# Attention slots of a second block: value tiles beside softmax rows, one output projection behind all slots

## The chip, the cores and the metric

The kernel runs on one core of one Trainium2 chip. The metric is the device time of one execution in microseconds (us). The program issues work to TensorE (PE, matmuls and its weight loads PEld), VectorE (DVE), ScalarE (ACT), GpSimd (POOL) and SyncE (SP, DMA issues). Each engine runs its own queue in program order, and they meet at semaphores.

## The reference, cut to what matters

Two model blocks stand one behind the other, for 512 tokens of width 1024 in fp32. The first (two layers of gated feed-forward and a mixer) is not touched by the change. The second takes its output, normalises it, projects it, and runs a state-space branch and an attention branch side by side:

```python
h = rmsnorm_2(x, norm_mix); proj = h @ w_in
z, xBC, dt_raw, qkv, gate_logits = split(proj)
y_ssm = mamba2_branch(z, xBC, dt_raw, ...) @ w_ssm_out     # dt = softplus(dt_raw + dt_bias), causal conv of xBC, 4 groups
q, k = rope(qkv[0]), rope(qkv[1]); v = qkv[2]               # 12 heads of 128: 3 groups of 4
# per group: window 128, 512 (dilation 4), 2048 (dilation 16), softmax over its window;
# the three groups of a head are merged by a softmax over their log-sum-exp
y_att = dilated_attention_branch(q, k, v) @ w_att_out       # 4 merged heads, 512 -> 1024
mixed = sigmoid(gates[0]) * y_ssm + sigmoid(gates[1]) * y_att
x = x + mixed @ w_mix_out; then a gated feed-forward and a last rmsnorm
```

## The kernel before, in words

**Weights.** All weights lie in one list of blocks of 128 x 1024 fp32 (512 KB), in the order in which they are used (`second_blocks`, L2510, and `slot_blocks`, L2485, put the second block's together). SP loads them into four `raw` buffers (L425). GpSimd splits each block into a rounded high part `w_hi` (L445) and a remainder `w_lo` (L448), in two buffers; a split begins when PE starts on the next block (semaphore `w_begun`). `product` (L495) multiplies one 128x128 tile of a block with 512 columns in three matmuls: high by high (L499), high by low (L503), low by high (L504). `project` is one block: eight products, 24 matmuls, into one PSUM bank of 128x512.

**Entry of the second block** (`second_mixer` of each engine). PE projects the dt tile into bank 5, adds up squares with a ones matmul (L518), projects three value tiles, with a second sum of squares between them. DVE forms two reciprocal roots (`first_rms`, `rstd`), the raw dt rows (L2263, L2265), scales the turn tables (L2268), scales and copies the value tiles to `att_vt` in residue order (L2037), then runs the softplus of dt (the "dt chain", L2273 to L2282, with ACT's exponential and logarithm), and clears `att_sum` (L2284).

**Slots.** A slot is one merged head: four of them, slots 0 to 2 in a loop, slot 3 behind it. Its steps:

- six tiles (three query, three key) into a ring of seven banks (5, 6, 7, 0, 1, 2, 3) with `tile_free` for each. DVE rotates each one: two products with the turn tables and a third (L2053 to L2055), then an add into `att_qk` (L2057);
- 12 transposes of the value tiles (L944), copied by ACT (L1452, behind a table load);
- four softmax rows r. Scores (L955, L958, banks r mod 2 and 2 + r mod 2), DVE's `shift` (scale and mask L2063 and L2065, maximum L2067, negation L2068), ACT's exponential (L1456), DVE's `over_sum` (L2073, L2074), PE's six transposes into banks 5 and 6 (L969), ACT's copies (L1463, L1465), and the mix of values in bank 7 (L979). Scores of r + 1 are issued ahead of the transposes of r; a value tile of the next slot (bank 4) stands between transposes and mix of r = 0, 1, 2. The softmax buffers are two deep;
- DVE normalises two of the eight tiles of x (`normalise`, L2046), ACT rounds the mixed output (L1471), DVE takes the remainder `att_lo` (L2089);
- PE waits for it and multiplies by this head's rows of `w_att_out` (`accumulate`, one block, eight bank results); DVE adds each to `att_sum` (L2027).

**Tail.** Behind slot 3 PE transposes the dt rows (L1134), ACT copies them and loads `sel`, and PE projects six state-space tiles into banks 5, 6, 7 in turn (`fill_bank`, `proj_free`). DVE scales each into `xbc_pad` (L2099) and runs a convolution of four taps (L2113 and three of L2116). Then come four state-space groups (`ssm_group`). Order is fixed by hand in every queue; no planner sets it.

Of the kernel before, what the change touches and what calls it, by code (L numbers as in the profile page):

```python
# [18 lines left out]
F32 = mybir.dt.float32  # L19
# [63 lines left out]
SLOT_STEPS = {  # L83
    "pe": {"w_split": 10, "tile_free": 9, "vt_ready": 3, "v_timed": 3, "soft_ready": 4, "soft_copied": 4,
           "soft_tail": 4, "soft_shifted": 4, "att_split": 1, "acc_free": 8, "qk_ready": 6},
    "act": {"v_turned": 3, "soft_shifted": 4, "soft_turned": 8, "att_mixed": 1},
    "dve": {"acc_free": 8, "tile_free": 9, "dve_step": 18, "tile_ready": 9, "soft_in": 4,
           "soft_shifted": 4, "soft_exp": 4, "soft_ready": 4, "att_rounded": 1, "att_split": 1,
           "acc_ready": 8, "qk_ready": 6},
}  # L90
# [76 lines left out]
def build(nc, io):  # L167
    ctx = ExitStack()
    with ctx:
# [11 lines left out]
        VALUE_BANKS = (3, SUM_BANK, 5)  # L181
# [93 lines left out]
        att_sum = sb("att_sum", [P, DC, T], F32, two_mem)  # L275
        ssm_sum = sb("ssm_sum", [P, DC, T], F32, two_mem)
# [17 lines left out]
        att_hi = sb("att_hi", [P, T], F32R, att_mem)  # L294
        att_lo = sb("att_lo", [P, T], F32R, att_mem)
# [71 lines left out]
        acc_ready, acc_free = sem("acc_ready"), sem("acc_free")  # L367
# [114 lines left out]
        def _(pe):  # L482
# [13 lines left out]
            def product(out, s, t, hi, lo, start, stop):  # L496

                hi_w, lo_w = w_hi[:, s, t * P:(t + 1) * P], w_lo[:, s, t * P:(t + 1) * P]
                first = nc.tensor.matmul(out, hi_w, hi, start=start, stop=False)  # L499
                if fresh[0]:  # L500
                    first.then_inc(w_begun, 1)
                    fresh[0] = False
                nc.tensor.matmul(out, hi_w, lo, start=False, stop=False)  # L503
                return nc.tensor.matmul(out, lo_w, hi, start=False, stop=stop)  # L504

# [400 lines left out]
            def accumulate(hi, lo, tiles):  # L906

                per = BLOCK // tiles
                for m in range(DC):
                    if m % per == 0:  # L910
                        s = take()
                    pe.wait_ge(acc_free, c.next(acc_free))
                    for k in range(tiles):
                        last = product(bank[m % 4][:], s, (m % per) * tiles + k, hi[k], lo[k],
                                       k == 0, k == tiles - 1)
                    last.then_inc(acc_ready, 1)

            def ring_tiles(n_tiles):
                for n in range(n_tiles):
                    if n == 3:  # L920

                        pe.wait_ge(acc_free, c.at(acc_free) + 4)
                    pe.wait_ge(tile_free, c.next(tile_free))
                    project(bank[RING[n % len(RING)]][:]).then_inc(tile_ready, 1)

            def value_tile(b):

                pe.wait_ge(tile_free, c.next(tile_free))

                pe.wait_ge(tile_free, c.at(tile_free) + len(RING) - 1)  # L930
                project(bank[b][:]).then_inc(tile_ready, 1)

            def attention_slot(more):

                pe.wait_ge(tile_free, c.at(tile_free) + len(RING))
                ring_tiles(2 * GROUPS)

                pe.wait_ge(vt_ready, c.next(vt_ready, GROUPS))
                for g in range(GROUPS):
                    if VALUE_BANKS[g] == RING[0]:  # L940

                        pe.wait_ge(tile_free, c.at(tile_free) + len(RING) + 1 - 2 * GROUPS)
# [3 lines left out]
                    last.then_inc(v_turned, 1)  # L946
                pe.wait_ge(v_timed, c.next(v_timed, GROUPS))

# [13 lines left out]
                scores(0)  # L962
                for r in range(RES):
                    if r + 1 < RES:
                        scores(r + 1)
# [6 lines left out]
                    if more and r < GROUPS:  # L972

                        value_tile(SUM_BANK)
# [8 lines left out]
                pe.wait_ge(att_split, c.next(att_split))  # L983
                accumulate([att_hi[:]], [att_lo[:]], 1)
# [14 lines left out]
            def out_block(waits=0):  # L999
# [4 lines left out]
                for m in range(2):  # L1004
                    to = fill_bank()
                    for k in range(4):
                        last = product(to[:], s, 4 * m + k, ssm_hi[:, k, :], ssm_lo[:, k, :], k == 0, k == 3)
# [108 lines left out]
            def second_mixer():  # L1116
                pe.wait_ge(tile_free, c.next(tile_free))

                project(bank[RING[0]][:], arriving=1).then_inc(tile_ready, 1)
                sum_squares()  # L1120
                for b in RING[1:1 + GROUPS]:
                    pe.wait_ge(tile_free, c.next(tile_free))
                    project(bank[b][:]).then_inc(tile_ready, 1)
                    if b == RING[1]:
                        sum_squares(1)
                with c.loop(3, SLOT_STEPS["pe"]):
                    attention_slot(True)
                attention_slot(False)
                pe.wait_ge(acc_free, c.at(acc_free) + 4)
# [9 lines left out]
                for n in range(SSM_TILES):  # L1139
# [1485 lines left out]
```

## Time and profile before

| what | value |
|---|---|
| runs, median | 3560.83 us (three: 3555.93 to 3565.5) |
| profiled execution | 3557.09 us, its span 3555.3 us |
| PE busy | 3309.0 us (93%) |
| DVE busy | 1814.8 us (51%) |
| POOL busy | 1827.6 us (51%) |
| ACT busy | 757.1 us (21%) |
| granted PE clock, mean | 0.969 of full |

The span is the time from the first to the last recorded instruction; the execution's own time has 1.8 us more. Busy PE time overstates PE's work, since matmuls overlap in their pipeline; a row's idle time and what ended it say more. "[2.44 <-DVE square_sum L1592]" behind a row reads: the engine sat idle for 2.44 us before it, and DVE's instruction at L1592 released it. "x12" is the number of instructions that a row stands for.

### The profile page before, as it was taken

What the parts mean: (1) busy time and instruction counts of PE and PEld (TensorE: products, weight loads), DVE (VectorE), ACT (ScalarE), POOL (GpSimd) and SP (SyncE); (2) the same over time, 40 slices, a digit from 0 to 9 for tenths busy, and PEclk for the clock granted to TensorE, in tenths of its full rate; (3) what the DMA queues carried; (4) which work ended last, traced back from release to release, by engine and by line L of the source; (5) the groups of instructions that cost most, each with busy time, mean ns of one, the idle gap of its engine ahead of it and who ended that gap; (6) DMA issues with size and microseconds to landing.
All of it is one profiled execution on the core that took longest, in us unless ns stands there. A gap on an engine that the chain in (4) does not pass through costs nothing.

```text
span 3555.3 us, 44605 instructions
## 1 busy us (share of the span) xinstructions
PE 3309.0 (93%) x14288; PEld 2589.9 (73%) x14288; DVE 1814.8 (51%) x2100; ACT 757.1 (21%) x1269; POOL 1827.6 (51%) x1026
## 2 busy tenths in 40 slices
PE   7999997899999999997889999888898899999997
PEld 5788774478887788874457888666776677778886
DVE  6541267663313733157654331755668866853313
ACT  2110124422201110013432210211113222222201
POOL 4556650056666646661036666433354445666664
PEclk9999998999999999998899999999999999999998
DMA  4223320023333223331013333321222222233332
GB/s 139 77 78 97 109 81 15 5 74 100 94 95 117 85 71 95 95 107 31 12 42 91 98 95 95 103 60 59 59 75 66 60 66 72 88 94 95 95 95 76
DMA packets 77138, 280.90 MB, mean 79 GB/s; under 512 B 9351, under 2 KB 9735, under 8 KB 76361
## 3 DMA queue, kind: packets, MB, share of 16 engines
q1 hardware_dynamic: 74016, 268.84, 25.1%
q10 hardware_dynamic: 2984, 10.27, 0.9%
q8 instruction: 82, 1.34, 0.2%
q14 instruction: 56, 0.45, 0.0%
HBM read 276.97 MB, written 2.10 MB: 78 GB/s over the span
## 4 chain that ended last, share of the span: by engine, by line
PE 78%; DVE 14%; issue 5%; ACT 2%; DVEq 0%; ACTq 0%; DMA 0%; SPq 0%
PE bank L499 23%; PE bank L504 23%; PE bank L503 23%; DVE xbc L2116 1%; PE bank L763 1%; PE bank L706 1%; PE bank L624 1%; DVE x_lo L1582 1%; PE bank L781 1%; DVE ssm_lo L1736 1%; DVE square_sum L1592 1%; DVE scaled L1947 1%; PE bank L979 1%; DVE y L1824 1%; DVE reach L2198 1%
## 5 line engine op out<-in xcount | busy, mean ns | idle before, releaser
L445 POOL TENSOR_SCALAR w_hi<-raw 128x1024 fp32r<-128x1024 f32 x504 | 551.2, 1094 | 1648.3 <-PE bank L499 1641.2
L448 POOL TENSOR_TENSOR w_lo<-raw,w_hi 128x1024 fp32r<-128x1024 f32 x504 | 1264.0, 2508 | 42.0
L499 PE MATMUL bank<-x_hi,w_hi 128*128 128x512 f32 x2896 | 1158.8, 400 | 83.2 <-DVE x_lo L1582 30.2
L504 PE MATMUL bank<-x_hi,w_lo 128*128 128x512 f32 x2896 | 1141.2, 394 | 0.0
L503 PE MATMUL bank<-x_lo,w_hi 128*128 128x512 f32 x2896 | 1140.9, 394 | 0.0
L499 PEld LDWEIGHTS bank<-x_hi,w_hi 128*128 128x128 f32 x2896 | 552.5, 191 | 224.3 <-issue 95.4
L503 PEld LDWEIGHTS bank<-x_lo,w_hi 128*128 128x128 f32 x2896 | 553.0, 191 | 118.9 <-issue 5.1
L504 PEld LDWEIGHTS bank<-x_hi,w_lo 128*128 128x128 f32 x2896 | 551.7, 190 | 118.2
L504 PE MATMUL bank<-hidden_hi,w_lo 128*128 (+1 forms) x880 | 347.6, 395 | 0.0
L499 PE MATMUL bank<-hidden_hi,w_hi 128*128 (+1 forms) x880 | 347.6, 395 | 0.0
L503 PE MATMUL bank<-hidden_lo,w_hi 128*128 (+1 forms) x880 | 347.6, 395 | 0.0
L1602 DVE SCALAR_TENSOR_TENSOR x<-bank,x 128x512 f32<-128x512 f32 x64 | 43.4, 686 | 561.8 <-PE bank L504 561.2
L1617 DVE TENSOR_TENSOR up<-bank,rstd 128x512 f32<-128x512 f32 x110 | 76.1, 692 | 396.5 <-PE bank L504 390.3
L1621 DVE TENSOR_TENSOR hidden_lo<-hidden,hidden_hi 128x512 f32 (+1 forms) x110 | 163.9, 1490 | 113.3 <-ACT hidden_hi L1185 113.3
L503 PEld LDWEIGHTS bank<-hidden_lo,w_hi 128*128 128x128 f32 x880 | 165.2, 188 | 40.2
L504 PEld LDWEIGHTS bank<-hidden_hi,w_lo 128*128 128x128 f32 x880 | 165.2, 188 | 40.1
L499 PEld LDWEIGHTS bank<-hidden_hi,w_hi 128*128 128x128 f32 x880 | 165.2, 188 | 40.1
L1169 ACT ACTIVATE x_hi<-x,gains 128x512 fp32r<-128x512 f32 x72 | 51.7, 718 | 644.2 <-DVE x L1602 643.3
L1185 ACT ACTIVATE hidden_hi<-hidden 128x512 f32 (+1 forms) x110 | 69.5, 632 | 477.5 <-DVE hidden L1619 477.5
L1183 ACT ACT_TABLE_LOAD x68 | 87.2, 1283 | 243.8 <-DVE gate L1615 243.8
L1619 DVE TENSOR_TENSOR hidden<-gate_silu,up 128x512 f32<-128x512 f32 x110 | 119.1, 1083 | 36.1 <-DVE up L1617 26.3
L1615 DVE TENSOR_TENSOR gate<-bank,rstd 128x512 f32<-128x512 f32 x110 | 76.1, 691 | 96.6 <-PE bank L504 86.3
(368 smaller groups left out, 3258.3 us busy)
## 6 DMA issues: line engine op xcount, KB each, us to landing
raw<-in_w SPq DMA_DIRECT2D x504, 512.0 KB, 3.6
dft<-in_dft ACTq DMA_DIRECT2D x2, 1536.0 KB, 6.8
x<-in_x SPq DMA_DIRECT2D x2, 1024.0 KB, 6.7
out<-x SPq DMA_DIRECT2D x4, 512.0 KB, 2.6
mask<-in_mask ACTq DMA_DIRECT2D x1, 1536.0 KB, 7.2
filt_cos<-in_dft_filter ACTq DMA_DIRECT2D x2, 512.0 KB, 6.5
filt_sin<-in_dft_filter ACTq DMA_DIRECT2D x2, 512.0 KB, 7.7
sel<-in_sel ACTq DMA_DIRECT2D x1, 768.0 KB, 4.4
```

The source lines that it names most:

```text
L445: nc.gpsimd.tensor_scalar(w_hi[:, s % 2, :], raw[:, s, :], 1.0, 0.0, ALU.mult, ALU.add).then_inc(w_rounded, 1)
L448: nc.gpsimd.tensor_tensor(w_lo[:, s % 2, :], raw[:, s, :], w_hi[:, s % 2, :].bitcast(F32), ALU.subtract).then_inc(w_split, 1)
L499: first = nc.tensor.matmul(out, hi_w, hi, start=start, stop=False)
L503: nc.tensor.matmul(out, hi_w, lo, start=False, stop=False)
L504: return nc.tensor.matmul(out, lo_w, hi, start=False, stop=stop)
L1169: nc.scalar.activation(x_hi[:, m, :], x[:, m, :], ACT.Copy, scale=g).then_inc(x_rounded, 1)
L1183: nc.scalar.activation(gate_silu[:], gate[:], ACT.Silu).then_inc(gate_activated, 1)
L1185: nc.scalar.activation(to, hidden[:], ACT.Copy).then_inc(hidden_rounded, 1)
L1615: link(nc.vector.tensor_tensor(gate[:], bank[2 * b][:], rstd[:], ALU.mult), gate_scaled)
L1617: link(nc.vector.tensor_tensor(up[:], bank[2 * b + 1][:], rstd[:], ALU.mult), pair_free)
L1619: link(nc.vector.tensor_tensor(hidden[:], gate_silu[:], up[:], ALU.mult), hidden_ready)
L1621: link(nc.vector.tensor_tensor(to_lo, hidden[:], to_hi.bitcast(F32), ALU.subtract), hidden_split)
```

## The change

- Entry: the first value tile is projected ahead of the first sum of squares, the third is split in two parts around the second. The sums go to banks 3 and 2. PE waits for no ring. DVE leaves the reciprocal of `first_rms` to slot 0 and scales the turn tables behind the value tiles. The dt chain, the logarithm of ACT and the clearing of `att_sum` leave this place.
- Slots: written out four times, no loops. Query and key tiles go to banks 0 to 5 without `tile_free`. Value transposes go to banks 6, 7, 3. The next slot's value tiles all use bank 4: tile 0 behind the value transposes, tile 1 behind the scores of rows 0 and 1, tile 2 between transposes and mix of row 2. In slot 3 the first state-space tile stands behind the scores of rows 0 and 1. Scores of r + 2 are issued behind the transposes of r.
- `att_hi` and `att_lo` have room for four heads, which share memory with tensors that are first written later. The output product of a slot is gone; behind slot 3 come one state-space tile and then four blocks of `w_att_out` that sum over all four heads in PSUM (`out_block`). DVE copies eight results to `att_sum` in place of 32 adds.
- The dt chain stands behind slot 3, with two convolutions and the first copies of the output between its steps. Four state-space tiles follow the dt transposes, not six.

```diff
             def attention_slot(j):
+                more = j < 3
+                for n in range(2 * GROUPS):
+                    if n == VALUE_TILE_BANK:
+                        pe.wait_ge(vt_ready, c.next(vt_ready, GROUPS))
+                    project(bank[n][:]).then_inc(tile_ready, 1)
+                pe.wait_ge(att_split, c.next(att_split))
+                pe.wait_ge(qk_ready, c.at(qk_ready) + VALUE_BANKS[2] + 1)
                 for g in range(GROUPS):
...
+                def beside(n):
+                    if more:
+                        if n:
+                            pe.wait_ge(vt_ready, c.at(vt_ready) + n)
+                        project(bank[VALUE_TILE_BANK][:]).then_inc(tile_ready, 1)
+                pe.wait_ge(qk_ready, c.at(qk_ready) + VALUE_TILE_BANK + 1)
+                beside(0)
                 pe.wait_ge(v_timed, c.next(v_timed, GROUPS))
                 pe.wait_ge(qk_ready, c.next(qk_ready, 2 * GROUPS))
...
                 scores(0)
+                scores(1)
+                if more:
+                    beside(1)
+                else:
+                    project(bank[VALUE_TILE_BANK][:]).then_inc(tile_ready, 1)
                 for r in range(RES):
-                    if r + 1 < RES:
-                        scores(r + 1)
                     pe.wait_ge(soft_ready, c.next(soft_ready))
...
-                    if more and r < GROUPS:
-                        value_tile(SUM_BANK)
+                    if r + 2 < RES:
+                        scores(r + 2)
+                    if r == 2:
+                        beside(2)
                     pe.wait_ge(soft_copied, c.next(soft_copied))
...
-                pe.wait_ge(att_split, c.next(att_split))
-                accumulate([att_hi[:]], [att_lo[:]], 1)
             def second_mixer():                                  # PE
+                project(bank[5][:], arriving=1).then_inc(tile_ready, 1)
+                project(bank[6][:]).then_inc(tile_ready, 1)
+                sum_squares(FIRST_SUM_BANKS[0])
+                project(bank[7][:]).then_inc(tile_ready, 1)
+                s = take()
+                project_part(bank[VALUE_TILE_BANK][:], s, 0, 2)
+                sum_squares(FIRST_SUM_BANKS[1])
+                project_part(bank[VALUE_TILE_BANK][:], s, 2, DC).then_inc(tile_ready, 1)
+                pe.wait_ge(both_means, 1)
+                pe.wait_ge(rms_ready, 3 * LAYERS + 1)
+                for j in range(4):
+                    attention_slot(j)
+                proj_tile()
+                pe.wait_ge(att_split, c.next(att_split))
+                for m in range(0, DC, 2):
+                    out_block(hi=att_hi, lo=att_lo)
                 pe.wait_ge(dt_done, c.next(dt_done, 2))
...
-                for n in range(SSM_TILES):
+                for n in range(2, SSM_TILES):
                     proj_tile()
             def attention_slot(j):                               # DVE, behind the six tiles
+                if more:
+                    value_tile(0, VALUE_TILE_BANK)
                 shift(0)
+                shift(1)
                 over_sum(0)
+                over_sum(1)
+                if more:
+                    value_tile(1, VALUE_TILE_BANK)
+                shift(2)
+                over_sum(2)
+                shift(3)
+                over_sum(3)
+                if more:
+                    value_tile(2, VALUE_TILE_BANK)
+                if j == 0:
+                    link(nc.vector.reciprocal(first_rms[:], first_rms[:]))
                 normalise(2 * j)
                 normalise(2 * j + 1)
...
-                add_outputs(att_sum)
+            def att_output(m):
+                b = bank[FILL[projected[0] % len(FILL)]]
+                projected[0] += 1
+                dve.wait_ge(proj_ready, c.next(proj_ready))
+                nc.vector.tensor_copy(att_sum[:, m, :], b[:]).then_inc(proj_free, c.add(proj_free))
             def second_mixer():                                  # DVE, behind the slots
+                link(nc.vector.tensor_scalar(u, e, 1.0, None, ALU.add), dt_log)
+                link(nc.vector.memset(xbc_pad[:, :, 0:SSM_TAPS - 1], 0.0))
+                dve.wait_ge(tile_ready, c.next(tile_ready))
+                link(nc.vector.tensor_tensor(xbc_pad[:, 0, SSM_TAPS - 1:], bank[VALUE_TILE_BANK][:], rstd[:],
+                                             ALU.mult))
+                conv_taps(0, 0)
+                conv_tile(1)
+                conv_taps(0, 1)
+                att_output(0)
                 dve.wait_ge(dt_magnitude, c.next(dt_magnitude))
                 link(nc.vector.tensor_scalar(spare, u, 1.0, None, ALU.subtract))
                 link(nc.vector.tensor_tensor(e, e, spare, ALU.subtract))
+                att_output(1)
                 link(nc.vector.reciprocal(u, u))
+                att_output(2)
                 link(nc.vector.tensor_tensor(e, e, u, ALU.mult))
                 link(nc.vector.tensor_tensor(log, log, e, ALU.add))
+                att_output(3)
...
+                for m in range(4, DC):
+                    att_output(m)
 def second_blocks(i):
...
+    first = group_tiles(w_x, w_b, w_c, 0)
+    out += first[0:2] + group_out(i["w_att_out_2"][0], 0) + first[2:]
```

## Rows read from the trace of the kernel before

**Rows 1.** Page, part 4: shares of the chain that ended last.
```profile
PE 78%; DVE 14%; issue 5%; ACT 2%; DVEq 0%; ACTq 0%; DMA 0%; SPq 0%
```

**Rows 2.** Windows: length; PE, PEld, DVE, ACT, POOL busy; PEclk, DMA share, GB/s.
```profile
2242.04:2271.87 29.83, 20.06 (x77) 14.86 (x77) 24.74 (x22) 12.02 (x17) 10.66 (x6) 0.92 0.35 131
2271.87:2361.70 89.83, 77.85 (x348) 63.15 (x349) 59.90 (x68) 11.64 (x22) 34.76 (x20) 0.89 0.20 59
2361.70:2444.44 82.74, 72.99 (x349) 59.57 (x348) 49.33 (x62) 11.06 (x21) 34.45 (x20) 0.96 0.21 59
2444.44:2526.16 81.72, 73.47 (x348) 59.84 (x349) 49.14 (x62) 11.06 (x21) 34.47 (x20) 0.96 0.21 63
2526.16:2595.28 69.12, 57.48 (x277) 46.16 (x275) 47.78 (x62) 11.05 (x21) 24.16 (x14) 0.95 0.18 54
2595.28:2632.21 36.93, 35.07 (x153) 28.84 (x153) 27.62 (x27) 6.10 (x9) 22.30 (x12) 0.95 0.34 104
```

**Rows 3.** PE's waits, 2240 to 2633 us: in total, times, longest.
```profile
PE bank L969 <- DVE soft L2074: 14.1, 5, 3.9
PE bank L955 <- DVE att_qk L2057: 10.5, 3, 5.5
PE bank L499 <- DVE att_lo L2089: 8.3, 4, 2.4
PE bank L979 <- ACT soft_t L1465: 6.2, 7, 0.9
```

**Rows 4.** Timeline of PE, entry and slot 3: start, length, idle before.
```profile
2244.47 1.12 PE L518 MATMUL bank<-square_sum,ones 128*128 128x512 f32 x2 [2.44 <-DVE square_sum L1592]
...
2254.11 2.08 PE L518 MATMUL bank<-square_sum,ones 128*128 128x512 f32 x2 [3.03 <-DVE square_sum L1592]
...
2271.87 0.76 PE L499 MATMUL bank<-x_hi,w_hi 128*128 128x512 f32 x1 [4.31 <-DVE att_vt L2037]
...
2562.47 1.13 PE L955 MATMUL bank<-att_qk 128*128 128x512 f32 x2 [2.15 <-ACT att_v L1452]
...
2570.86 2.90 PE L979 MATMUL bank<-soft_t,att_v 128*128 128x128 f32 x12 [0.71 <-ACT soft_t L1465]
```

**Rows 5.** Timeline of PE in mid-stream, slots 0 and 1.
```profile
2338.68 1.50 PE L979 MATMUL bank<-soft_t,att_v 128*128 128x128 f32 x12
...
2347.47 1.50 PE L979 MATMUL bank<-soft_t,att_v 128*128 128x128 f32 x12
...
2394.37 1.47 PE L944 MATMUL bank<-ident,att_vt 128*128 128x128 f32 x12
```

**Rows 6.** Timeline of POOL in slot 1.
```profile
2367.75 1.06 POOL L445 TENSOR_SCALAR w_hi<-raw 128x1024 fp32r<-128x1024 f32 x1 [1.94 <-PE bank L499]
2368.89 2.39 POOL L448 TENSOR_TENSOR w_lo<-raw,w_hi 128x1024 fp32r<-128x1024 f32 x1
2373.19 1.06 POOL L445 TENSOR_SCALAR w_hi<-raw 128x1024 fp32r<-128x1024 f32 x1 [1.91 <-PE bank L499]
```

**Rows 7.** Timeline of DVE on entry.
```profile
2247.76 6.30 DVE L1592 TENSOR_TENSOR square_sum<-square_sum,square 128x512 f32<-128x512 f32 x6
...
2274.46 3.34 DVE L2277 RECIPROCAL dt_rows<-dt_rows 32x512 f32<-32x512 f32 x1
```

**Rows 8.** Timeline of DVE, slots 1 and 3.
```profile
2369.71 2.53 DVE L2057 TENSOR_TENSOR att_qk<-rot 128x512 f32<-128x512 f32 x1
...
2575.57 0.69 DVE L2063 SCALAR_TENSOR_TENSOR soft<-bank,mask 128x512 f32<-128x512 f32 x1 [2.59 <-PE bank L958]
...
2580.03 0.69 DVE L2063 SCALAR_TENSOR_TENSOR soft<-bank,mask 128x512 f32<-128x512 f32 x1
```

**Rows 9.** Two lines' instructions: shortest, median, longest in ns.
```profile
L2057 DVE TENSOR_TENSOR att_qk<-rot x24: 1035/2526/3119, 2287.4 to 2561.2; 128x512 f32<-128x512 f32 x24
L2074 DVE TENSOR_SCALAR soft<-soft,soft_max x16: 619/620/1631, 2321.6 to 2583.8; 128x768 f32<-128x768 f32 x16
```

**Rows 10.** Groups of DVE, 2595 to 2632 us: busy, mean ns, idle before.
```profile
L2116 DVE SCALAR_TENSOR_TENSOR xbc<-xbc_pad,cols,xbc 128x512 f32<-128x512 f32 x13 | 17.3, 1332 | 0.5
```

More of the change, by code:

```diff
@@ L504, in product, with project_part @@
                 return nc.tensor.matmul(out, lo_w, hi, start=False, stop=stop)
+            def project_part(out, s, first, end):
+                for k in range(first, end):
+                    last = product(out, s, k, x_hi[:, k, :], x_lo[:, k, :], k == 0, k == DC - 1)
+                return last
             def project(out, arriving=0):
@@ L904, in _, with attention_slot @@
                 ffn()
[L906 to L938, printed above, removed]
+            def attention_slot(j):
+                more = j < 3
[5 more added lines that the diff above has]
+                pe.wait_ge(qk_ready, c.at(qk_ready) + VALUE_BANKS[2] + 1)
                 for g in range(GROUPS):
-                    if VALUE_BANKS[g] == RING[0]:
-                        pe.wait_ge(tile_free, c.at(tile_free) + len(RING) + 1 - 2 * GROUPS)
                     for t in range(RES):
@@ L1432, in second_mixer @@
                 act.wait_ge(sum_ready, c.next(sum_ready))
-                nc.scalar.activation(first_rms[:], bank[SUM_BANK][:], ACT.Sqrt, bias=eps[:], scale=1.0 / D
+                nc.scalar.activation(first_rms[:], bank[FIRST_SUM_BANKS[0]][:], ACT.Sqrt, bias=eps[:], scale=1.0 / D
                                      ).then_inc(rms_ready, 1)
@@ L1445, in second_mixer @@
                                      ).then_inc(dt_magnitude, 1)
-                act.wait_ge(dt_log, c.next(dt_log))
-                nc.scalar.activation(dt_rows[:, 3, :], dt_rows[:, 2, :], ACT.Ln).then_inc(dt_magnitude, 1)
-                with c.loop(4, SLOT_STEPS["act"]):
+                for j in range(4):
                     for g in range(GROUPS):
@@ L2019, in mixer @@
                 absorb(stage + 1, 1.0)
-            def add_outputs(total, first=False):
-                for m in range(DC):
-                    dve.wait_ge(acc_ready, c.next(acc_ready))
-                    if first:
-                        link(nc.vector.tensor_copy(total[:, m, :], bank[m % 4][:]), acc_free)
-                    else:
-                        link(nc.vector.tensor_tensor(total[:, m, :], total[:, m, :], bank[m % 4][:], ALU.add), acc_free)
             def by_residue(v):
@@ L2077, in attention_slot @@
                 shift(0)
+                shift(1)
                 over_sum(0)
-                for r in range(RES):
-                    if r + 1 < RES:
-                        shift(r + 1)
-                    if r + 1 < RES:
-                        over_sum(r + 1)
-                    if more and r < GROUPS:
-                        value_tile(r, SUM_BANK)
+                over_sum(1)
[9 more added lines that the diff above has]
+                    link(nc.vector.reciprocal(first_rms[:], first_rms[:]))
                 normalise(2 * j)
@@ L2283, in second_mixer @@
                      dt_done)
-                link(nc.vector.memset(att_sum[:], 0.0))
-                with c.loop(3, SLOT_STEPS["dve"]) as j:
-                    attention_slot(j, True)
-                attention_slot(3, False)
+                for m in range(4, DC):
+                    att_output(m)
                 dve.wait_ge(dt_timed, c.next(dt_timed))
                 link(nc.vector.memset(a_rows[:].bitcast(F32), 0.0))
-                link(nc.vector.memset(xbc_pad[:, :, 0:SSM_TAPS - 1], 0.0))
-                for k in range(SSM_TILES):
+                for k in range(2, SSM_TILES):
                     conv_tile(k)
```

96 lines of the change are left out of this document (38 added, 58 removed).

## The prediction

> **What bounds the kernel now.** I read the chain of waits first: TensorE (PE) holds 78% of it [rows 1], so time is won only where PE waits or runs below full clock. Then I cut the stretch that the change touches, from the first block's last product (2242.04 us) to the first state-space group (2632.21), into stages: entry, attention slots 0 to 3 (each with its output product), tail. They take 390.2 us, at a granted clock of 0.89 to 0.96 [rows 2]: part of it ran at 1.2 instead of 2.4 GHz. The list of PE's waits names what ends them: normalised softmax rows (14.1 us), rotated queries and keys (10.5), the rounding remainder att_lo of a slot's output (8.3), copies of turned probabilities (6.2 in 7) [rows 3]. PE's own timeline adds the entry (2.44, 3.03, 4.31) and shows what follows a wait: the mix at 2570.86, in slot 3 with its many waits, takes 2.90 us [rows 4], where one in mid-stream takes 1.50 [rows 5]. That is the lower clock.
>
> **What the stretch costs without waits.** In mid-stream GpSimd starts a new weight split each 5.44 us (2367.75, 2373.19), one a block [rows 6], so a projection tile, which is one block, is 5.44. From one mix to the next is 8.79 with a value tile inside [rows 5]: one softmax row (scores, transposes, mix) costs PE 8.79 − 5.44 = 3.35. The 12 value transposes show 1.47, of which 0.16 overlaps: 1.3 [rows 5]. The change keeps every block: 3 value tiles on entry, 24 query and key tiles, 9 value tiles, 4 blocks of output weights, 6 state-space tiles, 46 × 5.44 = 250.2; 16 rows 53.6; 4 × 1.3 = 5.2; two sums 1.8; dt transposes 0.7. Together 311.5, so 78.7 of the 390.2 us are waits and lower clock: the most that can be won.
>
> **Entry.** Now one tile stands ahead of the first sum, one and a quarter behind it, and no ring wait before slot 0. PE: 2242.0 + 5.4 + 0.9 + 5.4 + 1.4 = 2255.2. VectorE's (DVE) last six adds of squares end at 2254.1 [rows 7], and its chain begins 2.8 us later because the first sum does: 2256.9; up to 2259.5 if one more split falls on them. I take 2257.5: PE waits 2.4 (1.7 to 4.3), then 0.9 for the sum and 4.1 for three quarters of a tile: slot 0 begins at 2263 against 2271.87. The reciprocal of first_rms, the dt chain with its own (3.34 [rows 7]) and the memset of att_sum leave DVE's path to the first rotated tile. DVE still has the reciprocal of rstd (3.4), the dt rows, three value tiles and the turn tables, and comes to that tile some 3 us late. That lag ends at no wait of PE, since nothing in the six tiles waits for DVE.
>
> **A slot with a successor (0 to 2).** Value tile 0 covers the last rotation and ScalarE's (ACT) table load and value copies, for which PE waited 2.15 in slot 3 and more in the others [rows 3, 4]. Score sets 0 and 1 stand ahead of value tile 1. From a row's shift to the next is 4.46 in slot 3 [rows 8], the exponential's wait of 1.3 inside, and a normalisation is 0.62 [rows 9] with 0.2 for its reciprocal, which leaves a shift 2.3. From the end of scores 0 DVE needs two shifts and a normalisation: 5.5. PE has 1.35 + 5.44 = 6.8 of work: covered. And row 2 is ready 4.5 after scores 2, and PE has mix 0, transposes 1, scores 3, mix 1 = 4.65 meanwhile: covered by a hair. Row 3 lies under value tile 2. What stays is the last row's wait for its copies, 0.9 (6.2 / 7 [rows 3]). The wait of 2.2 to 2.4 us for att_lo goes: it is made under the next slot's first tile, and what is late next is nothing before the value transposes. Slot: 9 × 5.44 + 1.3 + 13.4 + 0.9 = 64.6; I take 65.1, three times 195.3. DVE is busy 49 us of 82 in slots 1 and 2 [rows 2], and eight adds of the output leave it: under 50 of 65.
>
> **Slot 3.** It has no value tiles; one state-space tile is put behind scores 1. The 2.2 after the value transposes stays [rows 4]; rows 0 and 1 are covered; row 2 waits 0.9 for copies; row 3 waits 1.6 (4.5 less transposes 0.66, copies 0.9, mix 1.34) and 0.9. 7 × 5.44 + 1.3 + 13.4 + 2.2 + 3.4 = 58.4.
>
> **Tail.** The output projection has the same 96 matmuls. DVE's 32 adds become 8 copies of 0.69, the time of a 128x512 read of a bank [rows 8]. Ahead of and between them DVE has two convolutions and the dt chain. A convolution is the bank's read and four steps of at most 1.33 on average [rows 10], 6.0 in all. PE fills three banks in turn with halves of 2.72. Counted from slot 3's last mix: att_lo and small steps 2.1, two convolutions 12.0, copy 0.7: bank free at 14.8, wanted at 13.6: wait 1.2. Then dt steps 1.8, copy 0.7, reciprocal 3.3, copy 0.7: free at 21.3, wanted at 20.2: wait 1.1. One tile 5.4, four blocks 21.8, these 2.3, transposes 0.7, dt_time 0.9, four tiles 21.8: 52.9. ACT's logarithm brings a table load more, which no PE work waits for; the load of sel comes behind dt_turned as before, beside four tiles. SP's weight queue and GpSimd's splits have the same number of blocks in another order: 0.
>
> **Unrolling.** PE, DVE and ACT now run the slots without a loop. Nearest rows: slots 0 to 2 (looped) and slot 3 (written out); the latter's chains are no longer [rows 4]. Gain inside covered chains: 0; code loading from 0 to 1 us a slot: I take 0.
>
> **Sum.** 21.0 + 195.3 + 58.4 + 52.9 = 327.6, plus 3 for lower clock. (Before, one minus the granted share times each stage's length is some 24 us, much of it while idle [rows 2]; waits over 2 us remain only on entry and in slot 3; bounds 0 and 8.) 330.6 against 390.2: −59.6. The profiled execution took 3557.1 us, span 3555.3 and 1.8 around it; it becomes 3497.5. The runs' median is 3.7 above it, so I say 3500. Its own range: 3489 to 3512.
>
> **The shared port, against this change.** The rotating add that starts at 2369.71 beside the split of 2368.89 + 2.39 takes 2.53 us and ends 0.96 behind the split's end [rows 6, 8]; at its shortest it takes 1.04, and a row's normalisation 0.62 or up to 1.63 [rows 9]. The Trainium skill, "SBUF — State Buffer", in its rule on the port pair that DVE shares with GpSimd, calls this an exclusive lock: the later one blocks for the whole instruction. The trace agrees: 0.96 is about the add's whole time alone. By that rule denser splits would lengthen DVE's covered chains by up to a split's 2.4 us each, which is rival A's mechanism; without any such meeting the sum stays as it is.
>
> **Rivals.** (A) Partly given back. A normalisation that meets a split is 1.0 longer [rows 9] and all behind it is later; 2 us twice in each slot (16), 8 more in the tail where convolutions and dt steps meet splits: +24, 3524. For it: row 2's cover has 0.1 us to spare. Against: these steps stand mostly where PE begins no block. 16%. (B) Waits only move, and all 78.7 come back: 3557. Against: each of the seven added covers holds 5.44 us of independent work. 3%. (C) Slower: DVE bounds the rotated tiles. It has them done in 4.9 of 5.44 us when the add meets a split (three steps of 0.7 and 2.5 [rows 8, 9]). If every add missed a split and waited for the next, a tile would cost DVE 10.9, and the six would lag 33 us per slot. It decides from 15 us of lag a slot (4 × 15 = the gain); at 17, 3497.5 + 68 = 3565. Against: once PE waits no split starts and the add takes 1.04, so the lag heals. By the port rule the same. 3%. (D) Weights come late: 0.5 MB in 5.44 us is 96 GB/s; the tail moved 104 [rows 2]. 3540, 1%. (E) No residual waits, full clock: 3487, 5%. My forecast: 72%.
>
> **How the numbers follow.** 8 in 10: 3486 to 3522, which leaves out most of A's far half, B, C, D and a little of E. No change means within 0.3%, about 10.7 us, the least a measurement of this kernel can tell. Faster: forecast, A, D and E, 94%; same, B, 3%; slower, C, 3%.
>
> **What would show it.** PE's waits in the stretch for DVE's soft rows fall from 14.1 to 2 to 4 us, for att_qk from 10.5 to under 1, for att_lo to 0; slots 65 us apart; granted clock near 1 in slots 0 to 2; two new waits near 1 us of an output half-block for a DVE copy. Wrong if a slot takes over 70 us, if tiles wait for weights, or if the tail takes over 58.

## The result, and the profile after

| | before | after |
|---|---|---|
| median | 3559.39 us (four runs, 3555.93 to 3565.5) | 3498.27 us (four runs, 3496.48 to 3501.54) |
| profiled execution, its span | 3557.09, 3555.3 | 3500.01, 3497.9 |
| PE, DVE busy | 3309.0, 1814.8 | 3284.9, 1804.6 |
| granted PE clock, mean | 0.969 | 0.977 |

Ratio of the medians 0.9831, 95% interval 0.9816 to 0.9845: 61 us faster. The forecast was 3500 (8 in 10: 3486 to 3522).

The windows of the changed kernel by stage, in the columns of [rows 2]: entry, slots 0 to 3, tail with the output projection.

```profile
2234.90:2259.18 24.28, 19.87 (x77) 15.04 (x76) 19.34 (x14) 7.95 (x11) 11.45 (x6) 0.93 0.43 160
2259.18:2325.86 66.68, 64.14 (x326) 53.05 (x324) 51.92 (x59) 11.81 (x23) 31.92 (x18) 1.00 0.23 72
2325.86:2392.63 66.77, 64.21 (x328) 53.12 (x326) 47.46 (x57) 9.66 (x20) 32.09 (x18) 1.00 0.22 71
2392.63:2459.39 66.76, 64.21 (x327) 53.12 (x326) 45.47 (x54) 9.67 (x20) 31.63 (x18) 1.00 0.23 71
2459.39:2519.02 59.63, 53.96 (x279) 44.21 (x278) 41.14 (x51) 9.66 (x20) 24.14 (x14) 1.00 0.20 62
2519.02:2572.34 53.32, 51.33 (x227) 40.91 (x226) 41.80 (x43) 8.49 (x12) 32.60 (x18) 1.00 0.30 94
```

The stretch takes 337.4 us where it took 390.2 [rows 2]: −52.7. The clock stands at 1.00 in all four slots. PE's waits in it (in total, times, longest), against [rows 3]:

```profile
PE bank L956 <- DVE soft L2054: 7.0, 5, 1.7
PE bank L518 <- DVE square_sum L1581: 4.4, 1, 4.4
PE bank L967 <- ACT soft_t L1452: 4.2, 5, 0.8
PE bank L938 <- DVE att_qk L2035: 2.1, 1, 2.1
PE bank L494 <- DVE att_sum L2116: 1.1, 2, 0.9
PE bank L494 <- ACT dt_time L1465: 0.9, 1, 0.9
```

Soft rows 14.1 to 7.0, rotated tiles 10.5 to 2.1 (slot 3 alone), att_lo 8.3 to none; the two sums' 5.5 became one wait of 4.4. All waits of over 0.15 us together fell from 53.2 to 19.7, by 33.5. The other 19.2 us of the 52.7 go with the clock (its mean in the stretch was 0.94 and is 0.99) and with what a wait costs beyond its listed time.

The spans differ by 57.4. The other 4.7 us lie outside the stretch: the changed kernel came to it 7.1 us ahead and lost 2.5 behind it. The code ahead of the stretch is the same in both. One place shows a part of it, the same PE work in the first block, before and then after, 20.40 us at a granted clock of 0.83 and 17.39 at 1.00:

```profile
1711.68:1732.08 20.40, 17.35 (x61) 9.45 (x59) 16.56 (x29) 9.75 (x20) 3.45 (x2) 0.83 0.18 53
```
```profile
1707.81:1725.20 17.39, 14.34 (x61) 8.75 (x59) 15.59 (x27) 8.78 (x18) 3.44 (x2) 1.00 0.21 62
```

### The profile page after: what moved, and what is told of

Read it like the earlier page. It is cut to its first block, busy times and chain, and to the rows that moved or that the text cites. A ratio compares the mean times of both kernels' runs of the same rounds, so it can differ in the third digit from the quotient of the medians.

```text
span 3497.9 us, 43803 instructions
## 1 busy us (share of the span) xinstructions
PE 3284.9 (94%) x14288; PEld 2575.5 (74%) x14288; DVE 1804.6 (52%) x2075; ACT 751.7 (21%) x1265; POOL 1832.2 (52%) x1026
## 4 chain that ended last, share of the span: by engine, by line
PE 80%; DVE 13%; issue 4%; ACT 2%; DVEq 0%; ACTq 0%; DMA 0%; SPq 0%
PE bank L494 24%; PE bank L499 24%; PE bank L498 24%; DVE xbc L2101 1%; PE bank L706 1%; PE bank L763 1%; DVE x_lo L1571 1%; PE bank L624 1%; DVE reach L2189 1%; PE bank L781 1%; DVE scaled L1936 1%; DVE square_sum L1581 1%; DVE y L1813 1%; DVE ssm_lo L1725 0%; PE bank L601 0%
## 5 line engine op out<-in xcount | busy, mean ns | idle before, releaser
L1591 DVE SCALAR_TENSOR_TENSOR x<-bank,x 128x512 f32<-128x512 f32 x64 | 43.5, 687 | 561.6 <-PE bank L499 561.0
```

## The experiments

Spans of different executions differ by such clock drops, so each kernel is judged twice: by its median against the kernel before, timed beside it, and by the **stretch**, the time from the start of GpSimd's weight split number 312 to that of number 368 (2207.78 to 2663.16 us before: 455.4). It is wider than the 390.2 us of [rows 2], and each kernel has the same blocks there. A repeat of the changed kernel gave the stretch to 0.01 us, the medians of its two sets differ by 4.

| kernel | median of its runs | ratio to before, 95% | stretch against before |
|---|---|---|---|
| changed | 3498.27 | 0.9831 (0.9816 to 0.9845) | −52.7 |
| e11, changed again | 3502.19 | 0.9848 (0.9826 to 0.9869) | −52.7 |
| e1, before without loops | 3542.7 | 0.9959 (0.9941 to 0.9976) | −10.7 |
| e2, output in the slots | 3517.81 | 0.9882 (0.9865 to 0.9898) | −37.8 |
| e2b, the same, dt later | 3516.76 | 0.9885 (0.9863 to 0.9907) | −37.5 |
| e3, row order undone | 3526.04 | 0.9908 (0.9891 to 0.9924) | −29.9 |
| e10, scores one row ahead | 3502.9 | 0.9842 (0.982 to 0.9864) | −49.6 |
| e4, entry undone | 3515.11 | 0.9872 (0.9855 to 0.9888) | −43.5 |
| e5, exponential 1 early | 3498.28 | 0.9826 (0.9803 to 0.985) | −59.6 |
| e6, e5 and tile 2 parted | 3490.15 | 0.9809 (0.9787 to 0.9831) | −63.2 |
| e7, second sum later | 3504.51 | 0.9849 (0.9829 to 0.9869) | −53.9 |
| e8, e6 and e7 | 3484.48 | 0.9798 (0.9776 to 0.9821) | −67.1 |
| e9, no remainder splits | 3492.51 | 0.9819 (0.9798 to 0.984) | −58.6 |

**e1.** The slot loops of the kernel before (slots 0 to 2 on PE and DVE, all four on ACT), written out.

```diff
-                with c.loop(3, SLOT_STEPS["pe"]):
+                for j in range(3):
```

> The kernel before, with its three inner slots written out instead of looped; nothing else changes. My theory of the forecast: the short pauses of 0.14 to 0.33 us that VectorE had between its steps in the looped slots come from the loop, and they go: per slot three exposed waits fall by 0.34, 0.63 and 0.66 us, 1.6 us in all, times 3 slots, so about 5 us less than before, 3554 us. Rival 1 (the loop itself was what the old slots lost): 15 us or more less, 3545 us or below. Rival 2 (longer code has its own price): no gain or slower than before.

Measured: 15 us by the medians, 10.7 by the stretch. The steps of a softmax row on DVE, in slot 0, looped and then written out:

```profile
2317.28 0.69 DVE L2063 SCALAR_TENSOR_TENSOR soft<-bank,mask 128x512 f32<-128x512 f32 x1 [3.20 <-PE bank L958]
2318.12 0.42 DVE L2065 SCALAR_TENSOR_TENSOR soft<-bank,mask 128x256 f32<-128x256 f32 x1
2318.69 0.95 DVE L2067 TENSOR_REDUCE soft_max<-soft 128x1 f32<-128x768 f32 x1
```
```profile
2315.15 0.69 DVE L2063 SCALAR_TENSOR_TENSOR soft<-bank,mask 128x512 f32<-128x512 f32 x1 [3.15 <-PE bank L958]
2315.88 0.42 DVE L2065 SCALAR_TENSOR_TENSOR soft<-bank,mask 128x256 f32<-128x256 f32 x1
2316.34 0.95 DVE L2067 TENSOR_REDUCE soft_max<-soft 128x1 f32<-128x768 f32 x1
```

A step begins 0.15 us behind the end of the one before it in the loop, 0.04 behind it now. PE's wait for att_lo in slots 1 and 2 went from 2.36 and 2.23 to 1.48. A slot from last mix to last mix went from 83.97 and 82.13 to 77.80 and 79.19; slot 0 gained 0.3 us, slot 3 1.3. The listed waits of slot 1 fell by 3.3 us; the rest of its 6.2 goes with the clock, 0.94 to 0.98. My theory named the right place and half the size; by the medians rival 1's bound is reached, but the loops are still a fifth of the change. The edit does not part DVE's pauses from what else went with the loops: ACT's table loads of 1.28 us ahead of the value copies, one a slot, go too, and a single one comes ahead of slot 0's first exponential. The load set no wait of note where it can be compared: in slot 3 PE waited 2.15 us for ACT's copies and now waits 2.11 at the same place for DVE.

**e2.** The changed kernel with the output product back in each slot.

```diff
+                pe.wait_ge(att_split, c.at(att_split) + 1)
+                s = take()
+                for m in range(DC):                     # PE, end of each slot
+                    if m >= 4:
+                        pe.wait_ge(acc_free, 8 * j + m - 3)
+                    product(bank[m % 4][:], s, m, att_hi[:, j, :], att_lo[:, j, :], True, True
+                            ).then_inc(acc_ready, 1)
...
+                for m in range(DC):                     # DVE
+                    dve.wait_ge(acc_ready, c.next(acc_ready))
+                    if j:
+                        link(nc.vector.tensor_tensor(att_sum[:, m, :], att_sum[:, m, :], bank[m % 4][:], ALU.add), acc_free)
...
```

> The changed kernel, with the output product back at the end of each of the four slots, its weight blocks moved back and the dt chain directly behind slot 3. My theory: each slot again waits for att_lo, 1.6 us times 4 = 6.3 us, some of it at a lower clock (2 to 3 us more), and the two waits of the joint projection (1.1 us) go: 5 to 9 us over the changed kernel, 3503 to 3507 us. Rival (the place of the output product is the main source of the whole gain): 15 to 20 us over it, 3513 to 3518 us.

PE's waits, 2225 to 2640 us:

```profile
PE bank L959 <- DVE soft L2062: 7.0, 5, 1.7
PE bank L495 <- DVE att_lo L2082: 6.7, 4, 2.3
PE bank L1132 <- DVE dt_rows L2286: 5.7, 1, 5.7
```

15.0 us over the changed kernel in the stretch: the rival's size. The waits for att_lo are what I named (6.7); three of the four lie in slots 1 to 3 and with their clock make 7.9 there. The other 7.1 lie behind slot 3: the fourth wait, and then DVE owes eight adds of the last output (5.78 us) and the dt chain, and PE has only one tile to do. In the changed kernel the 96 matmuls of the joint projection stand over this.

**e2b.** One tile more ahead of the dt transposes.

```diff
                 proj_tile()
+                proj_tile()
                 pe.wait_ge(acc_free, 32)
                 pe.wait_ge(dt_done, c.next(dt_done, 2))
...
-                for n in range(2, SSM_TILES):
+                for n in range(3, SSM_TILES):
                     proj_tile()
```

> As e2_output_in_slots (output product at the end of each slot), with one more tile of products ahead of TensorE's dt transposes, which waited 5.67 us in that run. It tells the output product's own price from that of the bare dt chain. My theory: 5.7 us of that run's 15 us over the changed kernel were the bare dt chain, so this one stands 8 to 9 us over the changed kernel in the stretch (3506 us). Rival (dt's wait only gives way to another at the next tile of the convolutions, VectorE being 10 us late): 13 us or more, 3512 us.

My theory fell. The dt wait shrank from 5.67 to 1.14 us and the first state-space matmul came 5.4 us earlier, and all of it was lost again at once: PE waits 1.4 and 2.9 us in the first group for DVE, and the clock goes to 0.92.

```profile
2586.80:2600.00 13.20, 13.11 (x64) 10.35 (x63) 12.81 (x12) 1.57 (x3) 7.98 (x4) 1.00 0.26 79
2600.00:2622.00 22.00, 17.70 (x80) 13.70 (x79) 13.26 (x18) 6.50 (x11) 10.20 (x7) 0.92 0.23 73
```

The stretch is the same within 0.3 us. DVE is the bound of that place (12.8 busy of 13.2), and another tile put ahead on PE does not mend that; 15 us is the worth of one projection behind all slots: the waits for att_lo, 24 adds less for DVE, and cover for dt.

**e3.** The order of rows as before, on PE (shown) and on DVE.

```diff
-                beside(0)
...
                 scores(0)
-                scores(1)
-                if more:
-                    beside(1)
...
                 for r in range(RES):
+                    if r + 1 < RES:
+                        scores(r + 1)
                     pe.wait_ge(soft_ready, c.next(soft_ready))
...
-                    if r + 2 < RES:
-                        scores(r + 2)
-                    if r == 2:
-                        beside(2)
+                    if r < 3:
+                        beside(r)
```

> The changed kernel, with the order of rows within a slot as before: scores of row r+1 ahead of the transposes of row r, value products between the transposes and the mix of rows 0 to 2, none behind the value transposes. My theory: per slot the waits are again 2.1 + 3.3 + 0.9 = 6.3 us where the changed kernel has 2.55, so 3.7 us times 3 slots and 1.5 us in slot 3, 13 us in all, and 3 to 6 us for a lower granted clock where it gives way: 14 to 20 us over the changed kernel, 3512 to 3518 us. Rival (this order is nearly the whole gain of some 50 us): 30 us or more over it, 3530 us.

PE's waits, 2225 to 2640 us, and the windows of slots 1 and 2 from last mix to last mix:

```profile
PE bank L950 <- DVE soft L2046: 13.2, 5, 3.2
PE bank L936 <- DVE att_qk L2029: 8.4, 4, 2.1
PE bank L961 <- ACT soft_t L1446: 5.0, 6, 0.8
```
```profile
2335.53:2407.28 71.75, 65.64 (x325) 54.30 (x325) 49.09 (x56) 9.78 (x20) 31.51 (x18) 0.98 0.21 66
2407.28:2480.57 73.29, 67.18 (x325) 55.40 (x325) 47.30 (x54) 9.78 (x20) 31.03 (x18) 0.95 0.21 65
```

22.9 us over the changed kernel, between my 14 to 20 and the rival's 30. The waits are those I named (2.1, 3.2 and 0.83 a slot). What I had too small is what a wait costs beyond its listed time: 3.56 us more of waits made a slot 5.0 longer at a clock of 0.98 and 6.5 at 0.95.

**e10.** The changed kernel, its value tiles where they are, the scores one row ahead; DVE's order follows.

```diff
                 scores(0)
-                scores(1)
                 if more:
                     beside(1)
...
                 for r in range(RES):
+                    if r + 1 < RES:
+                        scores(r + 1)
                     pe.wait_ge(soft_ready, c.next(soft_ready))
...
-                    if r + 2 < RES:
-                        scores(r + 2)
```

> The changed kernel with its value tiles where they are, but the scores of row r+1 only one row ahead, as before the change (scores r+1, transposes r, mix r). It parts the two halves of the row order that e3_row_order_undone took back together (25 us in the stretch). My theory: the place of the value tiles is nearly all of it; without them beside row 0, row 1 now waits 1 to 3 us where row 2 waited 1.7: 0 to 4 us over the changed kernel, 3498 to 3502 us. Rival (two rows ahead is what hides a row's chain of 4 to 5 us): 4 us more per slot and some lower clock, 12 us over it, 3510 us.

3.1 us over the changed kernel in the stretch, 0.5 in each of slots 0 to 2 and 1.6 in slot 3: within my theory's range, but not by its wait. No row waits 1 to 3 us for DVE in slots 1 and 2: row 2's 1.72 us is gone and each of three rows waits 0.83 for its copies. So of the 22.9 us of e3 (not the 25 that I wrote above) some 20 belong to where the value tiles stand and 3 to the second row of scores, if the two do not overlap.

**e4.** The entry as before: the first sum ahead of the first value tile, the second behind it, no parted tile, the dt chain, its logarithm and the clearing of att_sum ahead of the slots.

```diff
                 project(bank[5][:], arriving=1).then_inc(tile_ready, 1)
-                project(bank[6][:]).then_inc(tile_ready, 1)
                 sum_squares(FIRST_SUM_BANKS[0])
-                project(bank[7][:]).then_inc(tile_ready, 1)
-                s = take()
-                project_part(bank[VALUE_TILE_BANK][:], s, 0, 2)
+                project(bank[6][:]).then_inc(tile_ready, 1)
                 sum_squares(FIRST_SUM_BANKS[1])
-                project_part(bank[VALUE_TILE_BANK][:], s, 2, DC).then_inc(tile_ready, 1)
+                project(bank[7][:]).then_inc(tile_ready, 1)
+                project(bank[VALUE_TILE_BANK][:]).then_inc(tile_ready, 1)
```

> The changed kernel, with its entry as before: the two sums of squares early, whole value tiles, the dt chain and the table load ahead of the slots. My theory: VectorE comes some 17 us late to the first rotated tile, so TensorE waits about 8.6 us at slot 0's value transposes, the granted clock falls there (3 us), the sums wait 1 us and the tail gets 1.1 us less: 8.5 to 13.5 us over the changed kernel, 3507 to 3512 us. Rival (the slack of slot 0 takes it up): about 3 us over it, 3501 us.

9.3 us over the changed kernel in the stretch, 8.8 of it before slot 0's value transposes, where PE now waits 6.02 us for the last rotated tile it needs, and 2.2 behind them at a clock of 0.95; the tail is 1.7 shorter. The theory stands in place and total; its wait of 8.6 us was 6.0.

```profile
2307.11 0.45 PE L918 MATMUL bank<-ident,att_vt 128*128 128x128 f32 x1 [6.02 <-DVE att_qk L2033]
```

**e5.** What the trace after shows of row 2, slot 1 (start, length, idle before). DVE finished shift 1 at 2371.61, but ACT's exponential 1 begins at 2374.89:

```profile
2374.14 0.60 ACT L1450 ACTIVATE soft_t<-bank 128x512 f32<-128x512 f32 x1 [3.83 <-PE bank L956]
2374.63 0.38 ACT L1452 ACTIVATE soft_t<-bank 128x256 f32<-128x256 f32 x1
2374.89 0.94 ACT L1443 ACTIVATE soft<-soft,soft_shift 128x768 f32<-128x768 f32 x1
```
```profile
2376.02 0.16 DVE L2053 RECIPROCAL soft_max<-soft_sum 128x1 f32<-128x1 f32 x1 [3.45 <-ACT soft L1443]
2376.22 0.62 DVE L2054 TENSOR_SCALAR soft<-soft,soft_max 128x768 f32<-128x768 f32 x1
2376.88 1.07 DVE L2018 TENSOR_TENSOR att_vt<-bank,rstd 128x512 f32<-128x512 f32 x1
2377.79 0.67 DVE L2043 SCALAR_TENSOR_TENSOR soft<-bank,mask 128x512 f32<-128x512 f32 x1
```

In ACT's queue it stands behind the copies of row 0, which wait for PE. DVE then waits 3.45 us for it, with shift 2 queued behind. The experiment takes it ahead of those copies.

```diff
                     exponentials(0)
+                    exponentials(1)
                     for r in range(RES):
...
-                        if r + 1 < RES:
+                        if 1 <= r < RES - 1:
                             exponentials(r + 1)
```

> The changed kernel, with ScalarE's order within a slot exponential 0, exponential 1, copies 0, copies 1, exponential 2, copies 2, exponential 3, copies 3: exponential(1) no longer stands behind the copies of row 0, which wait for TensorE. My theory: the 1.72 us wait at row 2's transposes comes from that place in ScalarE's queue; it falls to about 0.4 us in slots 0 to 2 and the 0.82 us of slot 3 to 0.4: 4.4 us less than the changed kernel, 3494 us. Rival (VectorE's own chain from scores(2) to soft(2), or GpSimd beside it, sets the wait): the waits stay at 1.7 us, no difference.

Row 2's wait is gone in all four slots (listed waits for soft rows 7.0 to 1.1, the last row of slot 3), slots take 64.83 us, the stretch 6.8 less than the changed kernel, where I expected 4.4: I had left 0.4 of each wait. The medians of the two (3498.28; 3498.27 and 3502.19) do not part them: this rests on the stretch.

**e6.** Tile 2 dealt out over rows 2 and 3 as well.

```diff
+                    if r == 2:
+                        part(0, 3)                      # ahead of transposes 2
...
-                        beside(2)
+                        part(3, 6)
+                    if r == 3:
+                        part(6, DC)
```

> The kernel of the run before in this list, and the value tile of row 2 dealt out in three parts: three products ahead of the transposes of row 2, three between them and the mix, two by row 3. My theory: row 2's transposes get 2.1 us more cover and their wait goes to nothing, and the wait for the copies of row 3 (0.84 us) too: some 2 us less than the run before, 3491 to 3493 us. Rival (parts of a tile only move the wait to the row whose cover they take, 0.8 us each): no difference against the run before.

No wait is left in slots 1 and 2, whose windows are these; PE is busy in all of them:

```profile
2328.69:2392.34 63.65, 63.65 (x325) 53.01 (x325) 47.86 (x56) 9.56 (x20) 31.66 (x18) 1.00 0.24 75
2392.34:2455.99 63.65, 63.65 (x326) 53.00 (x325) 45.51 (x55) 9.56 (x20) 31.96 (x18) 1.00 0.23 75
```

3.6 us less than e5, more than the theory's 2. It also gives the price of a wait: a slot takes 63.65 with none, 64.83 with one of 0.83, 66.77 with 1.72 and 0.83. A short wait costs some 0.2 to 0.4 us beyond its listed time even at full clock; e10's three of 0.83 make a slot 67.31, 0.39 each.

**e7.** A whole tile ahead of the second sum. PE's waits for the roots, which stood ahead of slot 0, stand ahead of its third tile.

```diff
                 project(bank[7][:]).then_inc(tile_ready, 1)
-                s = take()
-                project_part(bank[VALUE_TILE_BANK][:], s, 0, 2)
+                project(bank[VALUE_TILE_BANK][:]).then_inc(tile_ready, 1)
                 sum_squares(FIRST_SUM_BANKS[1])
-                project_part(bank[VALUE_TILE_BANK][:], s, 2, DC).then_inc(tile_ready, 1)
```

> The changed kernel, with a whole value tile (5.7 us) ahead of the second sum of squares at the entry, instead of behind it. My theory: the 4.41 us wait for the second sum was only a lack of cover: it falls to about 0.3 us and the entry from 24.3 to 20 us: 4 us less, 3494 us. Rival (what hangs on the second sum, the normalised tiles and the first rotated ones, is then late for slot 0's value transposes): the wait comes back there, no difference.

The wait fell from 4.41 to 0.39, and slots 0 to 2 ended 4.0 us earlier in the profile, though 1.4 of waiting for a rotated tile came back behind slot 0's value transposes, where the rival had put all of it; the entry ran at clock 1.00, not 0.93. Then slot 3 took 62.2 us where it took 59.63, with the same waits and a lower clock:

```profile
2461.90:2524.10 62.20, 56.54 (x280) 45.95 (x278) 41.65 (x51) 9.67 (x20) 24.16 (x14) 0.96 0.19 60
```

So the stretch gained only 1.2, and the median (3504.51, all runs from 3501.3 to 3506.52) shows nothing won. Neither theory had the clock.

**e8.** Both edits together.

> The changed kernel with the edits of the two runs before this one together. My theory: they lie at different places and add up: 10 to 11 us less than the changed kernel, 3487 us. Rival (GpSimd's splits, 3.6 us for each block of weights, are what TensorE meets next): 5 to 6 us less, 3492 us.

14.3 us less than the changed kernel in the stretch: 10.4 from e6 and 3.9 from the entry, this time with slot 3 at clock 1.00. Median 3484.48, ratio to before 0.9798 (0.9776 to 0.9821), where the changed kernel has 0.9831 and 0.9848: the fastest version here.

**e9.** GpSimd leaves the low parts of 47 blocks unmade.

```diff
+                if not rest:
+                    pool.sem_inc(w_split, 1)
+                    return
                 nc.gpsimd.tensor_tensor(w_lo[:, s % 2, :], raw[:, s, :], w_hi[:, s % 2, :].bitcast(F32),
```

> The changed kernel, but GpSimd leaves out the subtraction that makes the low part of the weights (2.51 us each) for the 47 blocks of the stretch, so those low parts are old ones. It tells what GpSimd's long steps do to VectorE's. My theory (VectorE's two-input steps stretch beside GpSimd's): the six adds of the second sum fall from 9.04 to about 4.4 us and TensorE's 4.41 us wait there goes, the 2.67 us adds of the rotation fall to 1.04, and row 2's wait of 1.72 us stays, since it comes from ScalarE's queue: 5 to 6 us less than the changed kernel, 3493 us. Rival 1 (GpSimd's steps also set the row waits): those fall too, 10 us less, 3488 us. Rival 2 (the sharing costs nothing): no difference.

The six adds of the second sum in the timeline of DVE, changed kernel and this one, and then the rotating adds of both (shortest, median, longest in ns):

```profile
2243.39 9.04 DVE L1581 TENSOR_TENSOR square_sum<-square_sum,square 128x512 f32<-128x512 f32 x6
```
```profile
L2035 DVE TENSOR_TENSOR att_qk<-rot x24: 1036/2673/2743, 2267.0 to 2494.6; 128x512 f32<-128x512 f32 x24
```
```profile
2240.02 4.33 DVE L1588 TENSOR_TENSOR square_sum<-square_sum,square 128x512 f32<-128x512 f32 x6
```
```profile
L2042 DVE TENSOR_TENSOR att_qk<-rot x24: 1036/1101/1500, 2257.9 to 2484.9; 128x512 f32<-128x512 f32 x24
```

4.33 for 9.04, 1.10 for 2.67: both as expected, and the 4.41 us wait is gone. The softmax rows meet splits too, which the changed kernel's normalisations show beside those of e9:

```profile
L2054 DVE TENSOR_SCALAR soft<-soft,soft_max x16: 620/622/1591, 2305.1 to 2515.3; 128x768 f32<-128x768 f32 x16
```
```profile
L2061 DVE TENSOR_SCALAR soft<-soft,soft_max x16: 619/620/622, 2295.4 to 2507.3; 128x768 f32<-128x768 f32 x16
```

The long ones, 1.58 to 1.59 us, are row 3's in each of slots 0 to 2, beside the split that value tile 2 sets off; that tile also covers them. Slots 1 and 2 take 66.77 us as in the changed kernel, with the same 7.0 us for soft rows: GpSimd's long steps cost time in the entry and the tail, and none in a slot. Rival 1 falls. The stretch is 5.9 less: about 7.3 on entry and just ahead of it (a wait of 0.9 there goes too), 1.2 in the tail, less 2.6 in slot 3, where the clock drop of e7 is there again (62.23 us).

**e11.** The changed kernel again.

> The changed kernel itself, beside the others on one chip. My theory: its waits are the same to 0.02 us, and what differs from its first profile are drops of the granted clock in code that the change does not touch, in steps of 1.6 to 3.3 us: 3495 to 3502 us. Rival (the 7 us by which its first profile was ahead of the kernel before, ahead of the stretch, belong to the change): they are there again.

The stretch and every wait repeat. It came to the stretch 6.5 us ahead of the profile of before, which is what the rival said. But all kernels share that code, and the twelve others came to it between 0.6 and 9.5 us ahead, e1 with the kernel before's own design 4.0. Some 3.3 us of each lead (3.1 to 3.9) arise at the drop shown above, which only the profile of before has. So the lead is not of the new order. Whether it is chance is open: there is one profile of before, the only kernel with slot loops, and in 10 of the 13 sets the medians give more than the stretch, 3.8 us on average over all 13.

## Why the prediction was right

- **Time.** 3498.3 against 3500, with errors that cancel. In the stretch I forecast −59.6 and it was −52.7; the medians give 61. In the profiled pair 4.7 us lie outside the stretch, a part of them the clock drop shown above; the medians' share outside was not traced. The size of the change by itself is nearer 53 to 57 us (the stretch; the repeat's median). That is in the forecast's range, but the last 5 to 8 us come from where the forecast put nothing: luck.
- **Where the time went.** Taking back one part at a time costs 22.9 us for the order of rows, 15.0 for the output product, 9.3 for the entry; the loops are worth 10.7 in the kernel before. The sum, 58, is above 52.7: the parts overlap, the clock among them.
- **The base without waits.** 64.6 for a slot with 0.9 of wait in it, so 63.7: e6's slots take 63.65.
- **"Row 2 is covered by a hair."** This step failed: 1.72 us a slot, 0.82 in slot 3. Its cover was counted from scores 2 to soft 2 along DVE's chain and missed that the order in ACT's queue, which the change left as it was, ties exponential 1 to PE's transposes of row 0. e5 shows it by moving that one instruction. A slot is then 63.65, 2.55 of waits and 0.6 that waits cost beyond their listed time: 66.8 for the 65.1 forecast.
- **Entry.** Taken 21.0, measured 24.3. The wait is 4.41 where I took 2.4 with a bound of 4.3: two splits fell on the six adds, not one (9.04 us for 6.30 [rows 7]). The upper bound was nearly right, the choice wrong; e9 shows the cause. (The entry's own terms add up to 20.5, not 21.0.)
- **att_lo, dt, tail.** The att_lo waits went to nothing, the new waits for copies are 0.85 and 0.2 (1.2 and 1.1 forecast), the tail 53.3 for 52.9. The 2.2 kept in slot 3 is 2.1, though what ends it is DVE's last rotated tile and no longer ACT's copies; the closing list's "under 1" for att_qk had forgotten it.
- **Loops.** "Gain inside covered chains: 0" held for covered chains. Not for the exposed ones: [rows 4] showed slot 3's chain no shorter than the others' between PE's waits, but DVE's own rows had pauses of 0.15 us, and I did not read them. The bound of 0 to 1 us a slot for code loading came from no row; e1, the same kernel in longer code, shows no such price.
- **Rivals.** A's mechanism, a normalisation meeting a split, did occur, once a slot in slots 0 to 2 (1.6 us for 0.62). It was row 3's, under value tile 2, and cost nothing: e9's slots are as long without it. Its price on entry was real. B would have brought the waits back, C put tiles at 10.9 us, D made tiles wait for weights, E left no waits: none is in the traces.

The port rule that the prediction weighed shows most on DVE's adds of two inputs: the median rotating add goes from 2.67 to 1.10 us when GpSimd's subtraction is gone, while PE's waits for rows in the slots do not move. The six adds of the second sum, from 2243.39, lie over these two subtractions of the changed kernel:

```profile
2242.79 2.71 POOL L443 TENSOR_TENSOR w_lo<-raw,w_hi 128x1024 fp32r<-128x1024 f32 x1
2248.50 2.65 POOL L443 TENSOR_TENSOR w_lo<-raw,w_hi 128x1024 fp32r<-128x1024 f32 x1
```

Of the first 2.11 us are left when the adds begin, with the second 4.76; the adds take 4.71 longer than in e9. As "SBUF — State Buffer" of the Trainium skill has it under "Who interferes with whom", the later instruction waits out the other; the trace agrees for these adds.

**Open.** Why the clock drops in slot 3 in e7 and e9 and not in e8, whose entry is e7's. It costs about 2.6 us, and no kernel here was made to part the cases.

## What to carry to other kernels

Put independent work where a chain of another engine is exposed, and then read the queue of every engine in the chain: an instruction that the change left in place can tie the moved steps to what they were to be freed from. Where one place makes a vector engine late, do not move the wait but the work under it: the same 15 us stood in e2 and e2b at two places. Judge changes of under 10 us by a stretch with the same work at both ends, beside the median, for the clock moves whole runs by as much.

## What the runs showed of the hardware

- In a looped slot DVE's successive steps stand 0.15 us apart, written out 0.04. Writing out the loops of PE, DVE and ACT together was worth 10.7 us; how much of it is DVE's pauses was not parted.
- In the looped slots ACT loads a table (1.28 us) once a slot, four in all; written out, once in all four (e1).
- A granted clock below full follows waits, but not by their sum alone: e3's slots 1 and 2 have the same waits and clocks of 0.98 and 0.95; slot 3 has the same waits in the changed kernel and e7 at 1.00 and 0.96.
- Six adds of two 128x512 inputs take 4.33 us without GpSimd's subtractions and 9.04 beside two of them; a 128x768 normalisation 0.62 and 1.59.
